# Moving sixteen weight splits from GpSimd to ScalarE and VectorE, and writing out the loop over four recurrent heads

## What is computed

```python
qkv = silu(_dwconv_centred(concatenate([g_q, g_k, g_v], -1), gdn_conv_w))
gq = _l2norm(heads(gq)) * GDN_DK ** -0.5
gk = _l2norm(heads(gk))
...
decay = exp(where(tril, gc[..., :, None] - gc[..., None, :], -inf))
lower = where(strict, einsum('bhnid,bhnjd->bhnij', kb, k) * decay, 0.0)
sol = triangular_solve(lower + eye(c), rhs, lower=True, unit_diagonal=True)
...
def step(state, inp):
    v_new = u_i - einsum('bhcd,bhde->bhce', w_i, state)
    o = einsum('bhcd,bhde->bhce', qd_i, state) + einsum('bhij,bhje->bhie', attn_i, v_new)
    state = state * cd_i + einsum('bhcd,bhce->bhde', kd_i, v_new)
```

## Time and profile before

| quantity | value |
|---|---|
| median of 3 executions | 1608.91 us (1607.72 to 1609.78) |
| span of the profiled execution | 1607.6 us |
| PE busy | 1456.8 us (91%) |
| DVE busy | 934.6 us (58%) |
| ACT busy | 501.1 us (31%) |
| POOL busy | 495.5 us (31%) |
| DVE busy in one recurrent head (362 to 474 us) | 84.21 of 112 us |
| POOL busy in the same stretch | 17.09 us, 8 instructions |
| granted TensorE clock in the same stretch | 0.92 of full speed |

### The profile page before, as it was taken

The page is one execution under the profiler, slowest core; times in us unless marked ns, Lnnn a source line. Parts: engine busy times, 40 slices in busy tenths (PEclk is TensorE's granted clock), DMA queues, the critical chain, the costliest instruction groups (busy, mean ns, idle before and its releaser), DMA issues.

```text
span 1607.6 us, 20068 instructions
## 1 busy us (share of the span) xinstructions
PE 1456.8 (91%) x7078; PEld 1179.5 (73%) x7078; DVE 934.6 (58%) x1447; ACT 501.1 (31%) x906; POOL 495.5 (31%) x235
## 2 busy tenths in 40 slices
PE   7999999798898897889579999999999999996992
PEld 5777767686786786768348888888888888875871
DVE  4344458858859779669884444434444445258337
ACT  4333346155163263421252212222221211212125
POOL 4322212112112122025254434434433444533323
PEclk9999999899899998999889999999999999998996
DMA  7110101100101001001001111111111111111002
GB/s 225 40 40 27 40 14 32 40 14 32 26 14 44 13 27 45 1 27 53 26 13 48 44 52 52 39 52 52 39 52 52 43 49 52 42 50 34 31 14 105
DMA packets 44326, 68.18 MB, mean 42 GB/s; under 512 B 24048, under 2 KB 26736, under 8 KB 44272
## 3 DMA queue, kind: packets, MB, share of 16 engines
q1 hardware_dynamic: 43696, 66.46, 13.1%
q10 hardware_dynamic: 576, 1.05, 0.2%
HBM read 62.00 MB, written 5.51 MB: 42 GB/s over the span
## 4 chain that ended last, share of the span: by engine, by line
PE 70%; DVE 21%; issue 4%; ACT 3%; DMA 2%; DVEq 0%; SPq 0%; POOL 0%; ACTq 0%
PE banks L503 33%; PE banks L955 14%; PE banks L528 11%; DVE qkv L1539 2%; DVE outer L1605 1%; PE banks L636 1%; PE banks L792 1%; PE banks L872 1%; DVE mix L1846 1%; DVE mix L1775 1%; PE banks L658 1%; DVE inv L1608 1%; DVE d_n L1699 1%; PE banks L646 1%; DVE sum L1788 1%
## 5 line engine op out<-in xcount | busy, mean ns | idle before, releaser
L441 POOL TENSOR_TENSOR w_hi<-w_raw,one 128x1024 fp32r<-128x1024 f32 (+1 forms) x103 | 196.0, 1903 | 1030.5 <-PE banks L503 496.8
L503 PE MATMUL banks<-x_hi,w_hi 128*128 128x512 f32 (+1 forms) x912 | 366.5, 402 | 30.5 <-POOL x_lo L463 16.9
L503 PE MATMUL banks<-x_hi,w_lo 128*128 128x512 f32 (+1 forms) x912 | 358.8, 393 | 0.0
L503 PE MATMUL banks<-x_lo,w_hi 128*128 128x512 f32 (+1 forms) x912 | 358.8, 393 | 0.0
L1870 DVE SCALAR_TENSOR_TENSOR cv<-banks,fw,cv 128x511 f32<-128x511 f32 x176 | 131.9, 750 | 260.6 <-ACT cv L1331 252.8
L444 POOL TENSOR_TENSOR w_lo<-w_raw,w_hi 128x1024 fp32r<-128x1024 f32 (+1 forms) x103 | 263.7, 2560 | 8.1
L503 PEld LDWEIGHTS banks<-x_hi,w_hi 128*128 128x128 f32 (+1 forms) x912 | 172.8, 189 | 77.6 <-POOL x_lo L463 20.6
L503 PEld LDWEIGHTS banks<-x_lo,w_hi 128*128 128x128 f32 (+1 forms) x912 | 172.8, 189 | 37.8 <-issue 2.8
L503 PEld LDWEIGHTS banks<-x_hi,w_lo 128*128 128x128 f32 (+1 forms) x912 | 172.3, 189 | 38.0 <-issue 0.6
L1331 ACT ACTIVATE cv<-banks,fw_j 128x512 f32<-128x512 f32 x88 | 68.7, 780 | 333.6 <-PE banks L503 331.1
L955 PE MATMUL banks<-a_hi,w_hi 128*128 128x512 f32 x352 | 139.7, 397 | 18.8 <-DVE a_lo L1898 15.6
(11 more groups left out here) (226 smaller groups left out, 2143.4 us busy)
## 6 DMA issues: line engine op xcount, KB each, us to landing
w_raw<-w_all SPq DMA_DIRECT2D x102, 512.0 KB, 3.3
yT<-z_all SPq DMA_DIRECT2D x16, 256.0 KB, 2.0
mix<-xT SPq DMA_DIRECT2D x12, 256.0 KB, 8.0
bw<-rpb SPq DMA_DIRECT2D x8, 132.5 KB, 12.0
mix<-xT ACTq DMA_DIRECT2D x4, 256.0 KB, 5.9
inverse_dram<-inv SPq DMA_DIRECT2D x4, 256.0 KB, 2.2
packed<-inverse_dram SPq DMA_DIRECT2D x16, 64.0 KB, 2.6
cst<-consts SPq DMA_DIRECT2D x1, 848.0 KB, 10.6
```

Source lines behind the costliest of these rows:

```text
L441: nc.gpsimd.tensor_tensor(w_hi[u][:, 0:n], w_raw[ru][:, 0:n], one[:, :].to_broadcast([P, n]), ALU.mult).then_inc(w_high, 1)
L503: last = mm(ps[bank][0:cols, :], w[u][:, k * cols:(k + 1) * cols], seq(x[:, k, :], s), start=n == 0, stop=n == 3 * KT - 1)
```

## The change

In the recurrent stage sixteen chunks (15 to 30) are no longer split by POOL. ACT writes the high part (`high_w`) and DVE the low part (`low_w`), each at a fixed place in a head. POOL splits chunks up to 14 and goes on at 31. SP's program is the same, word for word. The loop over heads 0 to 2 is replaced by four written-out heads on PE, ACT and DVE.

```diff
@@ gpsimd
-            split_chunks(2, UP0)
+            split_chunks(2, GDN0 + 2)
+            split_chunks(OUT0 + 2, UP0)
@@ tensor
-            with pe.Fori(0, GH - 1) as h:
-                delta_head(h, False)
-            delta_head(GH - 1, True)
+            for h in range(GH):
+                delta_head(h, h == GH - 1)
@@ scalar
+            def high_w(c):
+
+                act_e.wait_ge(w_landed[raw(c)], 16 * (c // 2 + 1))
+                act_e.wait_ge(proj_done, 2 * c - 2)
+                nc.scalar.copy(w_hi[slot(c)][:, :], w_raw[raw(c)][:, :]).then_inc(head_high, 1)
...
                 silu(QX, 0)
+                high_w(GDN0 + 4 * h + 3)
...
                 gate(0)
+                high_w(GDN0 + 4 * h + 4)
...
                 turned_v(1)
+                high_w(GDN0 + 4 * h + 5)
...
                     for s in range(SEQS):
                         centre(h + 1, KX, s)
+                    high_w(GDN0 + 4 * h + 6)
@@ vector
+            def low_w(c):
+
+                dve.wait_ge(head_high, c - GDN0 - 1)
+                dve.wait_ge(w_ready, c)
+                TT(w_lo[slot(c)][:, :], w_raw[raw(c)][:, :], w_hi[slot(c)][:, :].bitcast(F32),
+                   ALU.subtract).then_inc(w_ready, 1)
...
+                low_w(GDN0 + 4 * h + 2)
                 log_decays(0)
...
                 step(nc.vector.memset(inv[:, 0, 0:IB * IB:IB + 1], 1.0))
+                low_w(GDN0 + 4 * h + 3)
                 dve.wait_ge(blocks_landed, 32 * h + 32)
                 eliminate()
...
                 dve.wait_ge(qd_ready, 4 * h + 4)
+                low_w(GDN0 + 4 * h + 4)
 
                 for m, landed in enumerate((d_landed, u_landed)):
...
                             between(lv + 1, s)
+                    if lv == 0:
+                        low_w(GDN0 + 4 * h + 5)
```

More of the change, by code:

```diff
@@ L68 @@
 HQ = 6 * 2 * SEQS * CH
-GDN_STEPS = 31
 ELIM_STEPS = 2 * (IB - 1)
@@ L248, in encoder_layer @@
         x_high, x_ready = sem("x_high"), sem("x_ready")
+        head_high = sem("head_high")
         dstep, astep, eps_set = sem("dstep"), sem("astep"), sem("eps_set")
@@ L434, in _, with split @@
         def _(pool):
-            def split(c, ru, u, landed, free, n=D):
+            def split(c, ru, u, landed, free, n=D, before=0):
                 pool.wait_ge(w_landed[ru], landed)
@@ L442, in split @@
                                         ALU.mult).then_inc(w_high, 1)
-                pool.wait_ge(w_high, c + 1)
+                pool.wait_ge(w_high, c + 1 - before)
                 nc.gpsimd.tensor_tensor(w_lo[u][:, 0:n], w_raw[ru][:, 0:n], w_hi[u][:, 0:n].bitcast(F32),
@@ L447, in split_one @@
             def split_one(c, free):
-                split(c, raw(c), slot(c), 16 * (c // 2 + 1), free)
+                split(c, raw(c), slot(c), 16 * (c // 2 + 1), free, before=4 * GH if c >= OUT0 else 0)
             def split_chunks(first, end):
@@ L457, in split_chunks @@
                         c = first + u
-                        split(2 * i + c, raw(c), slot(c), 16 * i + 16 * (c // 2 + 1), 4 * i + (2 * c - 2))
+                        split(2 * i + c, raw(c), slot(c), 16 * i + 16 * (c // 2 + 1), 4 * i + (2 * c - 2),
+                              before=4 * GH if first >= OUT0 else 0)
             def low_x1(s):
@@ L1260, in _ @@
                 centre(0, KX, s)
-            with act_e.Fori(0, GH - 1) as h:
-                delta_head(h, False)
-            delta_head(GH - 1, True)
+            high_w(GDN0 + 2)
+            for h in range(GH):
+                delta_head(h, h == GH - 1)
             for k in range(2, KT):
```

## The result

| | before | changed |
|---|---|---|
| median | 1609.35 us (1607.72 to 1610.58, 4 runs) | 1648.47 us (1645.41 to 1650.96, 4 runs) |
| ratio | 1 | 1.0248 (95% interval 1.0235 to 1.026) |
| span of the profiled execution | 1607.6 us | 1643.6 us |
| DVE busy | 934.6 us | 924.4 us |
| POOL busy | 495.5 us | 427.9 us |

The changed kernel is 2.5% slower. That is the forecast's sign and inside its range, 11 us above the predicted 1637. By the medians, 39.1 us apart, it lies just outside the band of +20 to +38 that the forecast itself stood for; by the profiled executions, 36.0 us apart, inside.

A forecast was written before the change was run, and what follows sets the result against it. DVE, with the transfers it waits for, was taken to bound each recurrent head from memset to first level. -29 + 11.3 - 2.8 + 17.9 + 24.6 + 6.4 = +28.4 us gave 1637 us, range 1617 to 1655.

The forecast's parts named there:

- the band of +20 to +38: Whole kernel: the slowdown in us that the main forecast stood for, given a chance of 0.60.
- What bounds the kernel: Recurrent heads, memset to first level: extra DVE time or a transfer landing after DVE arrives lengthens the head by as much.
- POOL's share: Four DVE operations per head, stretched while POOL works, return to normal length: 4 x 7.2 = -29 us.
- The subtractions: Low-part subtractions moved onto DVE, 1.26 us each with gap, partly covered by idle time: together +11.3 us.
- The jumps: DVE's loop jumps at the start of heads 1 and 2 vanish, 1.4 us gained each: -2.8 us.
- The cap by ACT: Start of heads 1 and 2: normed keys can't start before ACT's inverse roots, limiting the gain to 1.4 us per jump.
- ACT's copies: High parts written by ACT, 1.05 us each, mostly while ACT waits: costed at 0, upper end 3.2 us.
- The rings: DVE waits for transfers queued on SP behind loads that wait for DVE's subtractions: blocks +17.9 us, inverses +24.6 us.
- The load ahead: Small stores on SP queue behind 512 KB loads, 0.8 us each, eight times: +6.4 us, ends 0 and 9.6.
- A: Rival: the block and inverse round trips stay hidden and the kernel is faster, -20.5, 1588 us; chance 0.09.
- B: Rival: waits exposed but no queue cost, full 5.8 us from jumps, shorter DVE waits for PE: +12, about 1621 us; chance 0.14.
- C: Rival: SP's own jump (8.7 us), larger queue cost and ACT's fourth copy on the path: +43.5, about 1652 us; chance 0.13.

The follow-up runs named there:

- e2: The changed kernel with only SP's load of chunk +5 moved behind the block transfers; 1617.10 us, ratio 1.0052.
- e3: The changed kernel with only SP's load of chunk +6 moved behind the loads of the inverses; 1614.49 us, ratio 1.0038.
- e1: The changed kernel with SP's load of chunk +5 behind the block transfers and that of +6 behind the inverses' loads; 1583.24 us, ratio 0.9849.
- e6: The kernel before, loop written out, POOL splitting every chunk but +4 and +5 at other times, load of +6 behind the inverses' loads; 1576.41 us, ratio 0.9795.
- e4: The kernel before with only the loop over heads written out on PE, ACT and DVE; 1606.41 us, ratio 0.9986.
- e5: The changed kernel, both loads moved behind, SP's heads written out, block and inverse stores still waiting for the splits of +3 and +4; 1630.79 us, ratio 1.0145.
- e8: The changed kernel with the loads of chunks +5 and +6 cut to 256 KB instead of 512, timing only; 1641.73 us, ratio 1.0206.

## Why the prediction was right, point by point

**What bounds the kernel.** That DVE's line from the memset to the first level sets a head's length held: the waits taken out of it in e2 (30.4 us), e3 (33.3) and e1 (both) took 31.4, 34.0 and 65.2 us off the median.

**POOL's share, -29.** The elimination fell by 14.7 us over four heads, and no operation between it and the expansion is stretched either. e6 against e4 takes the same term out without any work added to DVE: 30.0 us by the medians, 28.0 by the spans. Cut into the stretches of the table, 13.4 of it lie in the elimination and 14.0 in both directions, 27.4 in all; the rest is of another kind, see the end.

**The subtractions, +11.3.** 1.22 us each, as taken. In line at +3 and +4. Head 3's +5 and the covered ones together cost less than was put down: the last stretch of the table changed by -0.4 against +1.2.

**The jumps, -2.8.** -3.0 in the table, and e4's median gives -2.1, with the 1.3 us in it by which e4's head 0 is longer. The cap by ACT was right: e4 shows the wait for the inverse roots.

**ACT's copies at 0.** Nothing of them is seen: the first stretch of heads 1 to 3 is 35.3 us both in the changed kernel and in e4, which has none.

**The rings, +17.9 and +24.6.** The mechanism was confirmed by e5, and the size came out somewhat small: DVE waits 23.2 and 25.0 us in all, where the working without the load's release, issue and gap gives 19.7 and 22.3. The first wait for inverses fits, 5.3 to 5.6 us against 5.4, and so do the blocks of heads 1 and 3, 4.96 and 4.94 against 4.9. In the changed kernel SP was released 0.18 us after DVE's subtraction, as after POOL's, and the store of the inverses went 0.56 us after it, where the working had 0.60. The block store went 0.84 to 0.89 us after it instead of 0.61; see the rivals.

**The load ahead, +6.4 with ends 0 and 9.6: this term was mis-sized.** On SP's rows the inverses' first load follows their store by 4.12 to 4.52 us in the changed kernel, 2.16 to 2.17 in e5 and e1; the blocks' follows by 4.50, 3.49, 4.50 and 3.44 in heads 0 to 3, where e1 has 2.17. So the stores land 2.0 to 2.4 and 1.3 to 2.3 us later, 15.6 us over the eight, instead of 0.8 each, and outside the bounds that the prediction gave. (The larger delays coincide with a fetch of code, see the end. The 17.7 us between e5 and the changed kernel are not this term alone: 5.5 us of them are the longer way to the store's issue.)

The step that failed is the subtraction 3.3 - 2.1 = 1.2, which took the difference of two landing times for the time that the load occupies the queue. The store of the inverses lands 2.0 us later although the load went 0.38 us before it, so on this reading 512 KB occupy the queue for about 2.4 us. A likely reason, which no run separates, is that a lone small store has data time of its own within its 2.1 us, so that the difference is too small by that much. The rows of before had no transfer behind another, and the upper bound should have been the whole landing time of the load less the gap, 3.3 - 0.44 = 2.9 us. With it the term's ends would have been 0 and 23. With the measured 15.6 in place of 6.4 the prediction's sum gives +37.6, against the 36.0 of the profiled executions.

The rule quoted from the Trainium skill (DMA: Bandwidth & Descriptors, section "Two DMAs through the same engine are not ordered") has two halves: descriptors of a queue start in order, and they are pipelined. The landings fit both. The small store is held up behind the load, and one after the other the two would have landed 3.3 - 0.4 + 2.1 = 5.0 us after the store's issue, where 4.2 was measured; so some 0.8 us overlap. The 0.8 that the prediction put behind the rule was my reading of two landings, not the page's.

**The rivals.** A, the faster kernel at 1588 us, is what e1 measured at 1583 once SP's order is changed: -25 us where the sum without the rings had -20.5, and SP's order decided the sign. The sum had missed that the subtraction of +3 then fills the old wait for the blocks: memset to block copy takes 5.2 us over four heads in e1 and 4.1 before, so the four subtractions cost 1.1 us there, not 5.0. B's gain in DVE's waits for PE didn't come (2.45 us in the second level as before). C named a jump of SP's. In the changed kernel the end of a loop stands between the load and the block store in every head, in head 0 that of `load_chunks`. In e8 head 0 has its load outside any loop, and its block store goes 0.56 us after the subtraction, in heads 1 to 3 0.87 to 0.91; so the jump costs about 0.3 us, 1.2 over four heads, and not 2.9 each. C's time of 1652 was near; its larger queue term pointed the right way, and its jump and its copy on ACT did not come.

## What to carry to other kernels

When a split, a copy or any other releaser of a buffer moves to another engine, walk through the DMA queue's program and ask of each transfer behind the released load who waits for it: here the new releaser was the very engine that needed the next transfer, and the ring cost 65 us where the change itself would have won 25. Keep latency-critical small transfers ahead of bulk loads in a queue, and bound the price of a load ahead by its whole landing time. Before moving work off GpSimd because it slows VectorE, see whether it can run beside operations that read PSUM: in e6 neither the convolution nor the scores grew by it.

## What the runs showed of the hardware that I had not expected

A 64 KB store of 64-byte pieces has two speeds. In e5, where no load is near, the block store of head 0 landed in 3.6 us and that of head 1 in 2.2. In the DMA view of 4 us around the first, the only other transfer is one of instructions (q8); in that of 2.5 us around the second there is none:

```profile
q1 hardware_dynamic: 1040, 0.07, 15.2%
q8 instruction: 1, 0.02, 1.7%
...
block_dram<-packed SPq DMA_DIRECT2D x1, 64.0 KB, 3.6
```

```profile
q1 hardware_dynamic: 1040, 0.07, 23.6%
...
block_dram<-packed SPq DMA_DIRECT2D x1, 64.0 KB, 2.2
```

The changed kernel has the same pattern: heads 0 and 2 with such a transfer beside the store wait 1.0 us longer for the blocks than heads 1 and 3 without. So a fetch of written-out code can fall on a transfer that is waited for. In head 0 of the kernel before a transfer of instructions comes too, but after the store's data, and the store lands in 2.1 us. This is a coincidence, not an experiment: no kernel was run in which the fetch alone was moved. It accounts for about 3 of the 5 us by which e5 missed its forecast.

In e6 a second gain came in that no part of the theory had. The first matmuls of the levels, sixteen of 128x128, ran at two speeds. PE in head 1 of the kernel before, then of e6 (start us, duration us, line; idle ahead in brackets):

```profile
417.96 3.75 PE L792 MATMUL banks<-x,u_t 128*128 128x128 f32 x16 [4.41 <-issue]
```

```profile
399.57 2.02 PE L802 MATMUL banks<-x,u_t 128*128 128x128 f32 x16 [0.90 <-issue]
```

Before, PE had idled 4.41 us and the granted clock over 414 to 422 us was 0.62 of full speed (between its two levels, 1.2 and 2.4 GHz); in e6, where chunk +4 is split later and its filler runs right before the level, PE had idled 0.90 us and the clock over 396 to 404 us was 1.00, the upper level (from the view of windows, whose last terms are the clock, the DMA share and GB/s):

```profile
414.00:422.00 8.00, 4.04 (x18) 3.98 (x19) 7.83 (x13) 0.84 (x2) 1.68 (x1) 0.62 0.21 66
```

```profile
396.00:404.00 8.00, 6.08 (x40) 5.29 (x41) 7.76 (x17) 1.47 (x3) 0.96 (x1) 1.00 0.22 68
```

The levels are then so much quicker that DVE's wait of 1.82 us is gone, and from the expansion to the next head heads 0 to 2 take 44.2 us instead of 45.4 to 45.9 in e4. In head 3 the corresponding stretch is 2.4 us longer than in e4, and the cause of that was not looked for.

Filler right ahead of the short matmuls isn't by itself enough for the upper level. In e1 too a filler runs right before the level. In its heads 0 and 2 the sixteen matmuls take 2.02 us. In its head 1 PE had waited 2.48 us ahead of that filler and 0.56 behind it, and they take 3.75, at the lower level, 0.50 of full speed:

```profile
399.80 0.50 PE L530 MATMUL banks<-x_hi,w_hi 128*128 128x512 f32 x1 [2.48 <-DVE w_lo L1570]
...
402.40 3.75 PE L794 MATMUL banks<-x,u_t 128*128 128x128 f32 x16 [0.56 <-issue]
```

```profile
402.00:404.50 2.50, 2.10 (x10) 2.13 (x11) 2.50 (x5) 0.02 (x1) 0.00 (x0) 0.50 0.29 110
```

From the expansion to the next head e1 takes 46.3 us in that head and 45.3 in heads 0 and 2, so within one kernel the slow matmuls go with 1.0 us. These were seen, not set up: no kernel moved the filler alone.
